# A two-layer hybrid trunk on one core: layers joined by token tile, conditioning sums spread over both merge loops

## The reference, cut to what matters

```python
ada = silu(c) @ ada_w[l] + ada_b[l]            # (1, 6 * 1024): twelve pieces of 512 columns
h = rms_norm(x) * (1 + scale1) + shift1         # pieces 0..3 are shift1, scale1
p = h @ w_in[l]                                 # q, k, v | mq, mk, mv, gates | mo | ga, gb
att = sliding_window_attention(...)             # window 128, 8 heads of 64
mem = mlstm_chunkwise(...)                      # 4 heads of 128
m = sigmoid(ga) * (att @ w_attn_up[l]) + sigmoid(gb) * (mem @ w_mlstm_up[l])
x = x + gate1 * (m @ w_out[l])                  # pieces 4, 5
h2 = rms_norm(x) * (1 + scale2) + shift2        # pieces 6..9
e = top-2 experts of the best of 4 groups       # 16 experts, width 512
x = x + gate2 * sum_k w_k * ffn_e(h2)           # pieces 10, 11
```

## Time and profile before

| what | value |
|---|---|
| median of 3 runs (1729.4 to 1733.0) | 1731.59 us |
| span of the profiled execution, first to last instruction | 1724.8 us |
| PE busy | 1506.9 us, 87% |
| DVE, ACT, POOL busy | 33%, 19%, 7% |
| mean granted clock of TensorE | 0.940 |
| DMA, mean | 213 GB/s |

### The profile page before, as it was taken

One profiled execution on the slowest core, in us unless ns is written; L12 is line 12 of the kernel. 1 busy time (PEld: TensorE's weight loads), 2 busy tenths in 40 slices (PEclk: granted clock), 3 DMA queues, 4 the chain that ended last, 5 costly groups with the idle time before them and its releaser, 6 DMA issues.

```text
span 1724.8 us, 18335 instructions
## 1 busy us (share of the span) xinstructions
PE 1506.9 (87%) x5819; PEld 669.3 (39%) x5820; DVE 563.9 (33%) x1459; ACT 323.4 (19%) x809; POOL 121.8 (7%) x157
## 2 busy tenths in 40 slices
PE   4999999999983999987749999999999387999982
PEld 1544444544441333332335444454444132333330
DVE  1346432446333212111134554243642411221213
ACT  3133411200011212111132343111000121221210
POOL 1100000011101000000111000000110100000001
PEclk8999999999996999999769999999999789999996
DMA  9822111055747899999952111113563799997984
GB/s 307 338 97 98 49 49 49 13 206 173 291 142 268 268 375 379 376 388 360 322 180 98 49 49 50 49 49 108 206 224 145 292 314 381 378 354 247 310 303 165
DMA packets 160813, 366.59 MB, mean 213 GB/s; under 512 B 12433, under 2 KB 14705, under 8 KB 160753
## 3 DMA queue, kind: packets, MB, share of 16 engines
q1 hardware_dynamic: 127568, 256.26, 42.2%
q0 software_dynamic: 21664, 83.89, 12.8%
q10 hardware_dynamic: 11520, 25.70, 5.0%
HBM read 334.37 MB, written 31.46 MB: 212 GB/s over the span
## 4 chain that ended last, share of the span: by engine, by line
PE 69%; DMA 11%; SPq 5%; DVE 5%; issue 4%; ACT 2%; POOL 2%; ACTq 0%; DVEq 0%; POOLq 0%; PEldq 0%
PE bank L939 23%; PE bank L1160 14%; PE bank L929 11%; PE bank L1105 6%; PE bank L1172 6%; DMA weight_ring<-in_w_up_dram 6%; DMA regA<-in_w_up_dram 2%; SPq L428 2%; SPq L431 2%; SPq L371 2%; DMA weight_ring<-in_ada_w_dram 1%; PE bank L1152 1%; PE bank L999 1%; POOL expert_rows L558 1%; PE bank L988 1%
## 5 line engine op out<-in xcount | busy, mean ns | idle before, releaser
L939 PE MATMUL bank<-h_features,weight_ring 128*128 128x512 f32 x768 | 342.4, 599 | 3.1 <-ACT regB L674 1.9
L1160 PE MATMUL bank<-weight_ring,merged_features 128*64 128x512 f32 x960 | 227.2, 628 | 35.3 <-DMA weight_ring<-in_w_up_dram 28.2
L939 PEld LDWEIGHTS bank<-h_features,weight_ring 128*128 128x128 f32 x768 | 144.8, 192 | 182.7 <-issue 182.4
L929 PE MATMUL bank<-weight_ring,h_features 128*128 128x512 f32 (+1 forms) x512 | 196.1, 541 | 1.7 <-ACT h_features L628 1.7
L1703 DVE TENSOR_TENSOR merged_features<-bank,merged_features 64x512 f32<-64x512 f32 x44 | 30.5, 693 | 381.8 <-ACT merged_features L809 381.8
L1160 PEld LDWEIGHTS bank<-weight_ring,merged_features 128*64 128x64 f32 x960 | 73.5, 144 | 165.4 <-issue 160.8
L929 PEld LDWEIGHTS bank<-weight_ring,h_features 128*128 128x128 f32 x512 | 96.0, 190 | 97.0 <-issue 91.6
L1160 PE MATMUL bank<-h_features,merged_features 128*64 128x512 f32 x256 | 117.1, 612 | 11.0 <-DMA regA<-in_w_up_dram 10.0
L1160 PE MATMUL bank<-regA,merged_features 128*64 128x512 f32 x256 | 117.5, 614 | 0.0
L1105 PE MATMUL bank<-weight_ring,merged_features 128*128 128x512 f32 x256 | 110.4, 593 | 3.0 <-POOL merged_features L538 3.0
L1172 PE MATMUL bank<-weight_ring,merged_features 128*64 128x512 f32 x480 | 109.6, 598 | 1.6 <-DVE merged_features L1689 1.6
(11 more groups left out here) (304 smaller groups left out, 1376.1 us busy)
## 6 DMA issues: line engine op xcount, KB each, us to landing
weight_ring<-in_ada_w_dram SPq DMA_DIRECT2D x24, 2048.0 KB, 8.7
weight_ring<-in_w_gate_dram SPq DMA_DIRECT2D x22, 2048.0 KB, 21.1
weight_ring<-in_w_down_dram POOLq DMA_DIRECT2D x22, 2048.0 KB, 14.9
weight_ring<-in_w_up_dram SPq DMA_DIRECT2D x22, 2048.0 KB, 20.4
weight_ring<-in_w_in_dram SPq DMA_DIRECT2D x18, 2048.0 KB, 8.9
h_features<-in_w_gate_dram SPq DMA_DIRECT2D x10, 2048.0 KB, 17.4
regA<-in_w_up_dram SPq DMA_DIRECT2D x10, 2048.0 KB, 27.4
regB<-in_w_down_dram POOLq DMA_DIRECT2D x10, 1536.0 KB, 11.5
```

The lines of the kernel that those rows point to most:

```text
L929: ins = te.matmul(bank[:, 0:w], hT[:, k, P * i:P * i + P], wv[:, k, :], start=(k == 0), stop=(k == KD - 1))
L939: ins = te.matmul(bank[:, :], wv[:, k, c0:c0 + P], rhs[:, k, :], start=(k == 0), stop=(k == kn - 1))
L1160: ins = te.matmul(ps[3][64 * part:64 * part + 64, :], xT[:, k, :], w[:, k, :], start=(k == 0), stop=(k == KD - 1))
```

## The change

- **Tiles instead of feature blocks between layers.** `h1T` leaves the two-bank order. Each token tile is transposed on its own (8 transposes into two banks of four, `h1_bank`), ACT evicts the low four feature blocks, DVE the high four (`h1_evac`). Tiles 0 and 1 are transposed and evicted first, PE then does q of tile 0, tiles 2 and 3, kv of tile 0, and so on. ACT and DVE evict tiles 0 and 1 ahead of the return to their loop's start, tiles 2 and 3 behind it.
- **No meeting of all engines.** The semaphores are split into those of the dense half and those of the expert half. SP resets one set while the other half runs, and engines only signal that they have left a half (`start_layer`, `start_experts`).
- **All twelve pieces in the merge loops.** Each layer sums pieces 4..11 of its own and 0..3 of the last layer (`STREAM`; the last layer sums the latter too, unused). DVE sums pieces n = 0..3 of that list by halves over the eight steps of the first merge loop, n = 4 behind it, n = 5..11 in steps 0..6 of the second. PE's sum over partitions and DVE's eviction stand behind ya 2, 4, 6, gb 0 and yb 0..7. In a step of the second loop the sum of the next piece now stands ahead of the eviction.
- **The room of x.** The pieces' weights go into `xs` ("x") and `regA` ("A"). `xs` is written to DRAM at the start of the layer (`x_kept`) and read back behind the last sum (`x_back`); DVE waits for it ahead of `wo`. A piece is loaded when the piece two before has been summed.
- **Slots.** Lower rows first: a token's two rows are told apart by slot number, not by rank of the gate; the gathers of the lower rows wait only for expert 14's last block, those of the higher ones for all. Gate weights are computed behind the tables.
- **Loads.** Expert buffers are assigned anew, three down loads go ahead of the experts where two did, `params` go behind the up load of expert 2. POOL scales the sum of squares ahead of its power in the boundary, which DVE did.

```diff
-G2_ADA = 10
-
-MID_ADA = {1: 4, 2: 5, 3: 6, 4: 7, 5: 8, 6: 9}
+
+STREAM = [(0, c) for c in range(HEAD_ADA, 12)] + [(1, c) for c in range(HEAD_ADA)]
+N_HALVED = 4
+ADA_AT = {("ya", 2): 0, ("ya", 4): 1, ("ya", 6): 2, ("gb", 0): 3, ("yb", 0): 4, ("yb", 1): 5, ("yb", 2): 6, ("yb", 3): 7,
+          ("yb", 4): 8, ("yb", 5): 9, ("yb", 6): 10, ("yb", 7): 11}
+ADA_SLOT = ("x", "x", "x", "x", "A", "x", "A", "x", "A", "x", "A", "x")
...
+                wait_reg(sp, head_xn, l * NT + NT)
...
+                sp.dma_start(xsave.rearrange("(i p) d -> p i d", p=P), xs[:, :, :]).then_inc(x_kept, 16)
...
+                through(sp, "mo", NT - 1)
+                load(l, "yb")
+                summed(sp, 0)
+                load_ada(1)
+                through(sp, "ga", 3)
+                load(l, "gb0")
+                summed(sp, 1)
+                load_ada(2)
+                summed(sp, 2)
+                load_ada(3)
...
+                through(sp, "ya", 7)
+                load_ada(4)
+                summed(sp, 3)
+                load_ada(5)
                 load_gate(0, 0)
...
+                through(sp, "hmT", NT - 1)
+                load(l, "wo0")
+                for n in range(6, len(STREAM)):
+                    summed(sp, n - 2)
+                    load_ada(n)
+                    if n == 7:
+                        load(l, "wo1")
+                    if n == 9:
+                        through(sp, "gb", 3)
+                        load_gate(1, 1)
+                summed(sp, len(STREAM) - 1)
+                sp.dma_start(xs[:, :, :], xsave.rearrange("(i p) d -> p i d", p=P)).then_inc(x_back, 16)
...
+                with sp.If(l < DEPTH - 1):
+                    sp.wait_ge(x_upd, NT)
+                    params(nxt)
+                wait_reg(sp, mix_done, l * 4 + 4)
+                for done in mix_sems:
+                    sp.sem_clear(done)
+                sp.sem_inc(mix_cleared, 1)
...
-                with sp.If(l < DEPTH - 1):
-                    params(nxt)
...
-                wait_reg(pool, y_out, nb * 32 + 32)
-                for i in range(NT):
-                    for k in range(2):
+                for k in range(2):
+                    wait_reg(pool, y_out, (nb if k else blocks_through(po, E - 2)) * 32 + 32)
+                    for i in range(NT):
...
-                    head_rows(l + 1)
-                    head_norm(l + 1, lambda i: act.wait_ge(combined, i + 1))
-                layer_end(act, l, share(2))
+                    start_layer(act, l + 1)
+                    wait_reg(act, mod_ready, l + 2)
+                    for i in range(NT):
+                        act.wait_ge(combined, i + 1)
+                        square(l + 1, i)
+                        wait_head(act, head_sq, l + 1, NT, i + 1)
+                        if i:
+                            normalise(l + 1, i - 1)
+                        if i >= 2:
+                            h1_evac(i - 2)
+                    normalise(l + 1, NT - 1)
...
+                def mod_sum(n):
+
+                    summed(pe, n)
+                    bank = take("ada", n)
+                    if STREAM[n][1] in (4, 5, 10, 11):
+                        ins = te.matmul(bank[:, :], ones[:, :], sum_buf(n), start=True, stop=True)
+                    else:
+                        ins = column_sums(bank, sum_buf(n))
+                    ins.then_inc(pj_ready, 1)
+
+                def h1_transposes(i):
+
+                    wait_reg(pe, head_xn, l * NT + i + 1)
+                    if i >= 2:
+                        pe.wait_ge(h1_low, i - 1)
+                        pe.wait_ge(h1_high, i - 1)
                     for k in range(KD):
...
+                h1_transposes(0)
+                h1_transposes(1)
                 for i in range(NT):
+                    pe.wait_ge(h1_low, i + 1)
+                    pe.wait_ge(h1_high, i + 1)
                     token_group("q", i, 512)
+                    if i == 0:
+                        h1_transposes(2)
+                        h1_transposes(3)
                     token_group("kv", i, 256)
...
+                def sum_ada(n, part=slice(0, KD)):
+
+                    ada_there(dve, n)
+                    acc, w = sum_buf(n), ada_home[ADA_SLOT[n]]
+                    for k in range(KD)[part]:
+                        if k == 0:
+                            link(ve.tensor_scalar(acc, w[:, 0, :], cz[:, 0, 0:1], None, ALU.mult))
+                        else:
+                            link(ve.scalar_tensor_tensor(acc, w[:, k, :], cz[:, k, 0:1], acc, ALU.mult, ALU.add))
+                    if part.stop == KD:
+                        ve.sem_inc(ada_summed, 1)
...
                     ve.scalar_tensor_tensor(merged[:, j, :], merged[:, j, :], 1.0, bank[:, :], ALU.add, ALU.mult).then_inc(free, 1)
+                    sum_ada(j // 2, slice(0, 4) if j % 2 == 0 else slice(4, KD))
+                    if ("ya", j) in ADA_AT:
+                        mod_chunk(ADA_AT["ya", j])
                 m_state(15)
                 m_finish(NT - 1)
+                mod_chunk(ADA_AT["gb", 0])
+                sum_ada(N_HALVED)
...
-                    if j - 1 in MID_ADA:
-                        mod_chunk(MID_ADA[j - 1])
-                    if j in MID_ADA:
-                        sum_mid(MID_ADA[j])
-
+                    if N_HALVED + 1 + j < len(STREAM):
+                        sum_ada(N_HALVED + 1 + j)
+                    mod_chunk(ADA_AT["yb", j])
+
+                wait_reg(dve, x_back, l * 16 + 16)
```

More of the change, by code:

```diff
@@ L34, with sums @@
 HEAD_ADA = 4
-G2_ADA = 10
-MID_ADA = {1: 4, 2: 5, 3: 6, 4: 7, 5: 8, 6: 9}
+STREAM = [(0, c) for c in range(HEAD_ADA, 12)] + [(1, c) for c in range(HEAD_ADA)]
[3 more added lines that the diff above has]
+ADA_SLOT = ("x", "x", "x", "x", "A", "x", "A", "x", "A", "x", "A", "x")
 def group_order(NT, NH, HM):
-    o = [("h1T", k) for k in range(8)]
+    def sums(name, i):
+        return [("ada", ADA_AT[name, i])] if (name, i) in ADA_AT else []
+    o = []
     for i in range(NT):
@@ L295, in mix_item @@
-            if name == "wo":
-                return lay(w_out, l)[:, 512 * part:512 * part + 512, :].rearrange("a (k p) n -> p (a k) n", p=P), D, 4
-            return cols8({"ya": w_attn_up, "yb": w_mlstm_up}[name], l, 0, D), D, 4
-        def slot(name, part, k, w):
-            return ring[:, ITEMS[ITEM[(name, part)]][2], 0:k * w].rearrange("p (k n) -> p k n", k=k)
-        def before(n):
-            return [it[2] for it in ITEMS[:n]].count(ITEMS[n][2])
+                return slot(name, 8, w), cols8(w_in, l, c0, w)
@@ L307, in of @@
+            if name in ("wo0", "wo1"):
+                r = 512 * int(name[2])
+                return slot(name, 4, D), lay(w_out, l)[:, r:r + 512, :].rearrange("a (k p) n -> p (a k) n", p=P)
+            return slot(name, 4, D), cols8({"ya": w_attn_up, "yb": w_mlstm_up}[name], l, 0, D)
         def of(w, l, e):
@@ L337, in ready, with h1_bank @@
             return pj[g % 2], pj_free[g % 2]
+        def h1_bank(i, half):
+            return ps[4 + 2 * (i % 2) + half]
         def wait_reg(eng, sem, value):
@@ new lines, in _ @@
+                sp.dma_start(xsave.rearrange("(i p) d -> p i d", p=P), xs[:, :, :]).then_inc(x_kept, 16)
+                sp.wait_ge(head_sum, HEAD_ADA)
+                for name in ("mqk0", "mqk1", "mv", "mo"):
+                    load(l, name)
+                wait_reg(sp, x_kept, l * 16 + 16)
+                load_ada(0)
+                with sp.If(l == 0):
+                    sp.wait_ge(zeroed, 3)
+                    sp.dma_start(xd.rearrange("(n p) d -> p n d", p=P),
+                                 zeros.unsqueeze(1).to_broadcast([P, ROWS // P, D])).then_inc(rows_zeroed, 16)
@@ new lines, in _ @@
+                through(sp, "q", NT - 1)
+                load(l, "ga0")
+                wait_reg(sp, moe_done, l * 4 + 4)
+                for done in moe_sems:
+                    sp.sem_clear(done)
+                sp.sem_inc(moe_cleared, 1)
+                through(sp, "mqk", 7)
+                load(l, "ga1")
+                through(sp, "mv", NT - 1)
+                load(l, "ya")
+                through(sp, "mo", NT - 1)
+                load(l, "yb")
+                summed(sp, 0)
+                load_ada(1)
@@ L1344, in _ @@
                 link(ve.tensor_scalar(wqk[:, 0, :], wqk[:, 0, :], HD ** -0.5, None, ALU.mult))
-                for k in range(0, KD, 2):
-                    bank, free = ready(dve, "h1T", k)
-                    ve.tensor_scalar(hT[:, k, :], bank[:, :], A1[:, k:k + 1], modc[:, k:k + 1], ALU.mult, ALU.add).then_inc(free, 1)
+                h1_evac(2)
+                h1_evac(3)
                 nh = HQ + HKV
@@ L1730, in _ @@
                     for i in range(NT):
-                        combine(i)
-                layer_end(dve, l, share(4))
+                        combine(0, i)
+                    for i in range(NT):
+                        combine(1, i)
```

(2 more changed lines are left out.)

501 lines of the change are left out of this document (244 added, 257 removed).

## The result

| | before | after |
|---|---|---|
| median of 4 runs each, us | 1730.5 | 1767.3 (1765.5 to 1768.3) |
| profiled span, us | 1724.8 | 1765.9 |
| mean granted clock | 0.940 | 0.934 |

The ratio is 1.0202, 95% interval 1.0183 to 1.0221. The forecast was 1725.5 and its range ended at 1739.

The account below looks back on a forecast made before the run. The chain was taken to go mostly over PE, with DMA pacing layer 0's experts. Savings of -38.7 and merge-loop costs of 2 x (6.3 + 8.3 + 1.7) = +32.6 gave -6.1: 1725.5 us, own range 1717 to 1731, whole range 1708 to 1739.

Parts of the forecast that it names:

- the one on the ya loop: First merge loop: DVE's half sums cost nothing, or 1 us if a chunk's finish meets one, besides PE's own sums.
- Boundary: Layer 0's experts to layer 1's q: q starts some 32 us behind the last product, not 61.0; -24, bounds -17 and -27.
- End: End of layer 1: only four gathers and one combine follow the last stores, so the last combine ends earlier; -7 us.
- Start: Start of layer 0: q starts after two tiles' transposes, -4.6, but runs partly at low clock, +2.2; -2.4 us.
- Routing: Gate-weight operations move behind the tables, covered by POOL's scatters, with one short operation fewer; -1.3 us per layer.
- Experts: Layer 0 only: DMA freed of params, 1.3, and of 0.5 MB of broadcast rows, 1.4; -2.7 us.
- Hand-over: Between ya 7 and yb 0: piece sums stand ahead of hmT's evictions, yb 0 at 20.5, not 18.05; +1.3 without PE's sum.
- Piece 5, +3.6, and its clock, +1.7: yb 0 to yb 1, no gb between: PE waits 3.6 us for DVE's sum; slow clock adds 1.7 per layer (0 to 2.7).
- The evictions behind the next sum: yb loop: DVE's eviction behind its next sum takes 8.5 against PE's 1.05 + 6.87; +1.5 us per layer.
- Rival C: x comes back late and PE stops behind two projection groups, both banks full; 1754 us, or 1739; chance 0.15.
- Rival A: Merge loops take the sums in, only PE's 6.3 stay: 1705 us, with some waits 1710; chance 0.20.
- Rival D: Every new PE pause slows its clock: three a layer at 2.7 make 16, not 3.4; 1738 us; chance 0.06.

Follow-up runs that it names:

- e3: The change with PE's three sums in the ya loop and their evictions left out; ya loop of layer 0 took 104.6 us.
- e1: The change with PE's three ya-loop sums moved from behind ya 2, 4, 6 to behind ya 3, 5, 7; 1731.6 us, 0.9995 of the kernel before.
- e5: The change with PE's ya sums behind odd steps, yb evictions ahead of DVE's next sum, gb j+2 behind yb j and its sum; 1716.4 us, ratio 0.9926.
- e2: The change with seven of the eight DVE operations of each of the first four sums left out; ya loop of layer 0 took 124.4 us.
- e7: e5 with DVE's piece 4 sum behind its yb evictions, PE's sum 4+j behind gb j+2, its eviction behind DVE's next sum; 1717.3 us, ratio 0.9912.
- e4: The change with one edit: in the yb loop DVE evicts PE's sum ahead of its next sum; 1758.9 us, ratio 1.0136.
- e8: e7 with piece 11 summed behind the last merge and first output-projection product, pieces 4 to 11 changing places; 1712.0 us, ratio 0.9904.

## Why the prediction was wrong

The step that failed is the one on the ya loop: "half a piece is 3.1 of DVE, and behind ya PE comes back to DVE only after a ga group (6.87). Nothing; 1 if a finish of a chunk (5.9) meets it." The first half is true, e3 shows it. The second half asked only when PE next needs a result of DVE. It did not ask whose bank the next group takes. That changes where a third group stands between two: from one that ACT has long freed to one that DVE frees behind the finish. It could be read in the code, in the parity of the groups; the rows show the loops only from 347 us on, and the argument rested on no row of the ya loop. Forecast 6.3 for PE's sums in the two loops, measured 43.6: 37.3 us, nearly all of the 47.2 that forecast (-6.1) and result (+41.1) differ by. e1 puts 34.4 of it on three entries of a table.

Point by point:

- **Boundary, -24.** Measured -26.3, q at 33.0 and not 32.0. Right. The first combine came 16.4 behind the product, 1.4 later than worked out, and q ran at full clock (7.05), where 2.2 had been taken off. No run shows the 4.4 us of slow start behind that 2.2.
- **End, -7.** -6.2, but not all by the step worked out. The last combine ended 29.7 us behind its product, where 26 was forecast and 33.4 stood before: 3.7. The gathers of the higher rows started 16.8 behind it and not 14.4. The other 2.4 came behind the last combine (3.9 us to the end of the span, before 6.3), which no term had.
- **Start, -2.4.** -8.4 in that profile. The mechanism was right, the 2.2 for a slow q was not needed, and 3.3 came from the head's last product. That part varies: in e5 the product waited 2.5 us for its weights, not 0.7, took 3.5, and q started at 44.8 instead of 43.3. In eight of the ten kernels that flow by tile it starts at 44.8 to 45.6, so some 2 of the 8.4 are luck of this execution.
- **Routing, -1.3 a layer.** With the output projection +2.1 and -0.7. Of the +2.1, 1.7 are the projection itself (56.9 us against 55.2, which it also takes in layer 1; the clock is at 0.50 for 3.4 us from 475 on), so routing gave +0.4 and -0.7: not seen in full. The pause of PE ahead of h2T's transposes is 4.60 us and was 2.75; PE's group of piece 10 (1.92) had stood in it, so that taking it out gave nothing, as forecast.
- **Experts, -2.7.** -3.5 in layer 0, but nine profiles with the parameters in the new place have from 272.7 to 276.8 us there. The difference is not evidence for the term. In layer 1 +3.6 came that no step had, and it is no accident of one execution (e1 has 14.9, e5 14.4): one pause of 14.8 us for the up weights of the sixth block, where before had two of 4.9 and 4.4 us for weights:

```profile
1506.45 1.08 PE L1236 MATMUL bank<-h_features,merged_features 128*64 128x512 f32 x1 [14.84 <-DMA regA<-in_w_up_dram]
```

  DMA's share is full (1.04) for 60 us around it in both. Which order of loads costs the 3.6 was not tried.
- **PE's six further sums, +6.3.** Six at 0.95 to 1.02 where no pause stands ahead. Right.
- **Hand-over.** yb 0 at 19.6 behind ya 7 against 20.5 forecast, and 17.9 before. Of the +1.7, 1.0 is PE's one sum there and 0.65 the wait for DVE's evictions, which start only behind piece 4's sum: right in kind, half the 1.3 forecast, since the sum ended 16.6 behind ya 7 and not 17.3. In e2, where piece 3's half is left out and piece 4's sum kept, the 0.65 are gone (18.9). In e5 and e7 PE has a second sum there and comes too late to wait. Its waits in the change, of which the first was 0.34 before:

```profile
379.92 1.23 PE L1166 MATMUL bank<-ident,weight_ring 128*128 128x128 f32 x8 [0.95 <-DVE regB L1647]
381.93 3.70 PE L1018 MATMUL bank<-regB,weight_ring 128*128 128x512 f32 x8 [0.79 <-DVE regB L1647]
```

- **Piece 5, +3.6, and its clock, +1.7.** 3.9 and 2.9. Right in kind.
- **Piece 6, +1.9.** It did not come: DVE started its sum at 395.13, right behind the merge and without a wait for its load, and PE's sum at 408.26 has no pause ahead.
- **The evictions behind the next sum, +1.5.** 4.3 as pauses and 1.2 at them, 5.5, under-sized by more than three times. Of the 6.9 that e4 gives back the other 1.5 belong to piece 5. That the sum of both terms (3.4) lies nearer is luck.
- **The copy of x.** x is back in time: at the output projection PE waits only 1.5 us for POOL's last merge, as before. Rival C did not come.
- **Rival A** (the merge loops take the sums in, 1705 to 1710) is near what the reordered kernels e5, e7 and e8 give: 1710.6 to 1717.3. **Rival D** put the clock's price on every new pause at 2.7; here the three pauses of the ya loop cost 5.9 together, 2.0 each, besides their own 11.0. With the yb loop's 2.9 that is 8.8 of clock a layer where the forecast had 1.7: D's 16 in all was the better size, but on other pauses than D had. The ones that cost clock are the four of 3.4 to 3.9 us, three of which no case held, and the five of 0.5 to 1.2 cost none in layer 0. The Trainium skill, "TensorE: Matmul & The Clock Gate", Part 1, has the slow clock as the default that activity releases; the trace agrees at each of the three pauses (0.74, 0.72 and 0.53 over the 6 us from 281, 313 and 345; 1.00 over the same stretches in e1).

## What to carry to other kernels

When groups of work share buffers in turn, adding a group changes which engine frees the buffer of every later one: write down, for each group behind the new one, whose buffer it takes and what its owner is doing then, before adding up durations. An engine at 42% busy can stop another for 11 us a loop by being late three times, and a move of the added group by one step costs nothing and took 36.8 of the ya loops' 43.6 us back (34.4 in the whole). And a gain just ahead of a stage with DMA at its full share needn't reach the total: e8's 4 us were there in the loop and not in the whole; that the loads are the reason is argued, not shown.

## What the runs showed of the hardware

The first operation of a sum on DVE (one tensor input, 128x512 from SBUF to SBUF) takes 0.48 us in the ya loop. In the yb loop, where POOL's addition of two SBUF tensors runs beside it, it takes 1.53 in the change and 1.22 in e5, where an eviction of 0.16 comes in between. e5, DVE and POOL:

```profile
426.98 1.22 DVE L1427 TENSOR_SCALAR regP<-regA,c_padded 128x512 f32<-128x512 f32 x1
```

```profile
426.65 1.26 POOL L600 TENSOR_TENSOR merged_features<-merged_features,regU 128x512 f32<-128x512 f32 x1 [10.20 <-DVEq L1655]
```

In both it ends 0.3 us behind POOL's operation (e5: 428.20 against 427.91; the change: 411.00 against 410.71), though it started 0.02 us behind POOL in one and 0.33 in the other: it waits for all of POOL's operation. Every such operation of both kernels that starts while one of POOL's runs ends 0.28 to 0.29 us behind it; in e5's yb loop the one at 382.32 has none of POOL's beside it and takes 0.49. The Trainium skill, "SBUF — State Buffer", section "SBUF: two separate sides", says that a pair of ports is locked for a whole instruction by whichever of the two engines starts first, and names DVE's faster modes among what needs it; the rows agree. The forecast had used this rule in the other direction only.
